# Queries, keys and values of both layers with seven block products instead of eight for some row pairs

## The reference, cut to what matters

```python
for l in range(DEPTH):                                    # two layers
    h = _rms_norm(x, norm_g[l])
    proj = jnp.einsum('bsd,de->bse', h, w_in[l])          # 256 x 2048 times 2048 x 6208
    q_a, k_a, v_a, z_a, c_q, c_kv, k_r, z_b = jnp.split(proj, split_points, axis=-1)
    ...                                                   # q_a, k_a, v_a: 1024 columns each
    o_a = _diff_attention(qa, ka, va, lam, rel_bias_table)
    ...
    x = x + jnp.einsum('bse,ed->bsd', mixed, w_out[l])
return second_block(...)
```

## Time and profile before

| | |
|---|---|
| median of 3 runs | 1946.02 us (1945.85 to 1946.25) |
| profiled execution | 1946.43 us |
| its span in the profile | 1944.6 us |
| PE matmul busy | 1928.8 us, 99% |
| DVE busy | 1371.4 us, 71% |
| ACT busy | 1047.4 us, 54% |
| granted TensorE clock, mean | 0.998 |

### The profile page before, as it was taken

The page is one execution under the profiler, slowest core; times in us unless marked ns, Lnnn a source line. Parts: engine busy times, 40 slices in busy tenths (PEclk is TensorE's granted clock), DMA queues, the critical chain, the costliest instruction groups (busy, mean ns, idle before and its releaser), DMA issues.

```text
span 1944.6 us, 27002 instructions
## 1 busy us (share of the span) xinstructions
PE 1928.8 (99%) x9818; PEld 1635.5 (84%) x9818; DVE 1371.4 (71%) x1941; ACT 1047.4 (54%) x1533; POOL 46.4 (2%) x73
## 2 busy tenths in 40 slices
PE   8999999999999999999999999999999999999997
PEld 7888888888888888888888888888888888888886
DVE  7755675656655675656768766888877887888787
ACT  5533676654433676664544544555555555555554
POOL 1000030000000020000100000000000000000000
PEclk9999999999999999999999999999999999999999
DMA  8666545556666555545666545565656566676653
GB/s 310 205 194 194 151 145 160 151 157 186 187 194 192 146 162 174 153 151 180 213 193 188 158 164 186 182 193 184 194 185 193 185 189 188 191 240 203 219 188 117
DMA packets 246964, 357.06 MB, mean 184 GB/s; under 512 B 15318, under 2 KB 136496, under 8 KB 246364
## 3 DMA queue, kind: packets, MB, share of 16 engines
q1 hardware_dynamic: 245148, 349.08, 58.3%
q0 software_dynamic: 1584, 6.54, 1.0%
q10 hardware_dynamic: 144, 0.26, 0.0%
HBM read 352.69 MB, written 3.16 MB: 183 GB/s over the span
## 4 chain that ended last, share of the span: by engine, by line
PE 98%; DMA 1%; DVE 1%; ACT 0%; issue 0%; SPq 0%; ACTq 0%
PE acc L410 22%; PE acc L387 16%; PE acc L389 15%; PE acc L388 15%; PE acc L403 11%; PE acc L1249 3%; PE acc L1250 3%; PE acc L1248 3%; PE aux L467 2%; PE aux L964 1%; DMA sb_stage<-w_kv 1%; PE aux L1249 1%; PE aux L1250 1%; PE aux L1248 1%; PE aux L982 1%; PE aux L945 1%
## 5 line engine op out<-in xcount | busy, mean ns | idle before, releaser
L350 DVE TENSOR_TENSOR sb_w_lo<-sb_stage,sb_w_hi 128x1024 fp32r<-128x1024 f32 x567 | 694.3, 1227 | 377.0 <-ACT sb_w_hi L345 369.9
L345 ACT ACTIVATE sb_w_hi<-sb_stage 128x1024 fp32r<-128x1024 f32 x567 | 598.5, 1058 | 501.5 <-PE acc L389 248.9
L410 PE MATMUL acc<-sb_xT,sb_w_hi 128*128 128x512 f32 x1856 | 445.7, 391 | 0.0
L410 PEld LDWEIGHTS acc<-sb_xT,sb_w_hi 128*128 128x128 f32 x1856 | 340.8, 188 | 65.8
L387 PE MATMUL acc<-sb_w_hi,sb_xT 128*128 128x512 f32 x768 | 305.7, 398 | 0.0
L389 PE MATMUL acc<-sb_w_hi,sb_xT 128*128 128x512 f32 x768 | 299.5, 390 | 0.0
L388 PE MATMUL acc<-sb_w_lo,sb_xT 128*128 128x512 f32 x768 | 299.3, 390 | 0.0
L403 PEld LDWEIGHTS acc<-sb_xT,sb_w_lo 128*128 128x128 f32 x1856 | 238.7, 191 | 9.3
L403 PE MATMUL acc<-sb_xT,sb_w_lo 128*128 128x256 f32 x1856 | 243.0, 283 | 0.0
L387 PE MATMUL acc<-sb_w_hi,sb_mT 128*128 128x512 f32 x560 | 224.7, 401 | 0.8 <-DVE sb_mT L490 0.7
L389 PE MATMUL acc<-sb_w_hi,sb_mT 128*128 128x512 f32 x560 | 218.6, 390 | 0.0
(11 more groups left out here) (335 smaller groups left out, 1910.5 us busy)
## 6 DMA issues: line engine op xcount, KB each, us to landing
sb_stage<-w_in SPq DMA_DIRECT2D x248, 512.0 KB, 3.9
sb_stage<-w_up SPq DMA_DIRECT2D x176, 512.0 KB, 3.7
sb_stage<-w_out SPq DMA_DIRECT2D x96, 512.0 KB, 4.2
sb_stage<-w_down SPq DMA_DIRECT2D x60, 512.0 KB, 7.0
sb_pair_stage<-w_down SPq DMA_DIRECT2D x28, 512.0 KB, 6.9
sb_stage<-w_kv SPq DMA_DIRECT2D x16, 512.0 KB, 6.8
sb_stage<-w_ukv SPq DMA_DIRECT2D x16, 512.0 KB, 4.0
sb_stage<-w_uq SPq DMA_DIRECT2D x12, 512.0 KB, 3.6
```

The costliest lines, as they stand in the source:

```text
L345: act.activation(w_hi[:, j % RING, 0:size], stage[:, j % RING, 0:size], ACT.Copy).then_inc(hi_ready, 1)
L350: dve.tensor_tensor(w_lo[:, j % RING, 0:size], stage[:, j % RING, 0:size], w_hi[:, j % RING, 0:size].bitcast(F32), ALU.subtract).then_inc( ...
L410: mm = pe.matmul(acc[:, 2 * pair + c, :], hi[:, k, c * P:(c + 1) * P], both, start=first and k == 0, stop=last and k == 3)
```

## The change

In each third (queries, keys, values: 1024 columns, two chunks) some row pairs are multiplied as a 2x2 block product in Winograd's form: the blocks of the left side are row tile x token block, those of the right side row tile x 512 columns. In the first third pairs 0 and 1 go this way, in the other two pairs 0, 1 and 2; that is 8 of 24 per layer. Such a "seven" takes the place of two ordinary units (one in each chunk) and is four units long in the counters: `seven0` to `seven3`, with 2, 1, 2 and 2 block products of three passes each. There are then 64 units in the stage, of which 32 are ordinary ("rows").

- New on SP: the weights of a seven are loaded by two DMAs of 512 KB into one of two pair slots (in `kvb`).
- New on DVE: four sums of 128x512 weights for each seven; `mix_x`, the sums of x blocks, 3 times 7 instructions per layer, placed in the memory stage before layer 0 and in the output projection before layer 1; `add_sevens_qkv` once and `add_rows_qkv` twice per third, in place of two `evacuate_scaled`.
- New on ACT: a copy of `m_first` per third, and `scale_qkv` (two instructions per chunk), since DVE no longer applies the norm's factor.
- Units of this stage are prepared five ahead, in six slots (two of them in `mT`). The last ones are prepared three ahead again.
- The loop over keys and values is written out.
- PE waits at a seven for `mixed_ready`, `tb_free` and `m_free`, and after the stage for `m_free` and `qkv_scaled`.

```diff
+QKV_ITEMS = [[[2, 3, 4], 0, [5], 1, [6, 7]]] + 2 * [[[3, 4], 0, [5], 1, [6], 2, [7]]]
...
+def qkv_ahead(u):
+
+    first = {0: [3], 1: [4], 2: [5], 3: [6, 7], 4: [8, 9]}
+    last = {U_QKV - 5: [], U_QKV - 4: [], U_QKV - 3: [U_QKV], U_QKV - 2: [U_QKV + 1], U_QKV - 1: [U_QKV + 2]}
+    return first.get(u, last.get(u, [u + QKV_RING - 1]))
...
+        def round_qkv(act, layer, j):
...
+            if kind == "seven2":
+                act.wait_ge(qkv_sums_ready, 2 * n + 1)
+            if kind == "seven3":
+                act.wait_ge(qkv_sums_ready, 2 * n + 2)
+            act.wait_ge(unit_used, base + max(0, j - QKV_RING + 1))
...
+        def rest_qkv(step, dve, layer, j):
...
+            dve.tensor_tensor(lo, src, hi.bitcast(F32), ALU.subtract).then_inc(lo_ready, 1)
+            if QKV[j][0] == "seven1":
...
+                dve.wait_ge(lo_ready, base + (j + 1))
+                step(dve.tensor_tensor(b11, b11, b12, ALU.add))
+                dve.tensor_tensor(b12, b12, b22, ALU.add).then_inc(qkv_sums_ready, 1)
+                dve.wait_ge(qkv_sums_ready, 2 * n + 1)
+                step(dve.tensor_tensor(b22, b11, b22, ALU.add))
+                dve.tensor_tensor(b21, b22, b21, ALU.add).then_inc(qkv_sums_ready, 1)
...
+                    def load_qkv_pair(n):
...
+                        if n >= 2:
+                            sp.wait_ge(lo_ready, base + (QKV_SEVENS[n - 2] + 4))
...
+                    def qkv_seven(j):
...
+                        pe.wait_ge(lo_ready, base + (j + 1))
+                        qkv_passes(m_first, near(0, 0), j, 0, first, last)
+                        qkv_passes(acc[:, 2, :], mixed(2), j, 1).then_inc(unit_used, 1)
+                        pe.wait_ge(lo_ready, base + (j + 2))
+                        qkv_passes(acc[:, 0, :], near(1, 0), j + 1, 0).then_inc(unit_used, 1)
+                        pe.wait_ge(lo_ready, base + (j + 3))
+                        qkv_passes(m_fifth, mixed(0), j + 2, 0, first, last)
+                        qkv_passes(m_seventh, mixed(3), j + 2, 1, first, last).then_inc(unit_used, 1)
+                        pe.wait_ge(lo_ready, base + (j + 4))
+                        qkv_passes(m_sixth, mixed(1), j + 3, 0, first, last)
+                        qkv_passes(acc[:, 1, :], near(1, 1), j + 3, 1).then_inc(unit_used, 1)
...
+                    def add_sevens_qkv(third):
+                        dve.wait_ge(m_copied, 3 * layer + third + 1)
+                        step(dve.tensor_tensor(inner_f, m_sixth, qkv_part(2 * third, 0), ALU.subtract))
+                        step(dve.tensor_tensor(outer_f, inner_f, m_seventh, ALU.subtract))
+                        dve.tensor_tensor(qkv_part(2 * third + 1, 0), m_fifth, inner_f, ALU.add)
+                        dve.tensor_tensor(qkv_part(2 * third + 1, 1), m_fifth, outer_f, ALU.add).then_inc(m_free, 1)
...
+                    for j in range(U_QKV):
+                        if j - 1 in QKV_END:
+                            add_rows_qkv(QKV_END.index(j - 1))
+                        if j - 4 in QKV_LAST_SEVEN:
...
+                            add_sevens_qkv(third)
+                        for ahead in qkv_ahead(j):
...
                         if j in (2, 3):
                             turn_scale(dve, tb0 + (j - 2), gain0 + (j - 2), par[:, bass.ds(layer * KT + 12, 4)])
                             turn_rest(dve, turn0 + (j - 2), token_part(xT, 3, j - 2, 0), token_part(xT, 3, j - 2, 1))
                         if j == 4:
                             x_rstd(step, dve, layer * SQ_PRO + SQ_PRO)
```

More of the change, by code:

```diff
@@ L73 @@
 U_MEM = 16
[L74 removed]
+U_QKV = 64
+U_LAYER = U_QKV + 32 + 32 + 32
 U_MIX = 14 * 4
@@ L149, with qkv_units @@
 DOWN_RING = 6
+QKV_ITEMS = [[[2, 3, 4], 0, [5], 1, [6, 7]]] + 2 * [[[3, 4], 0, [5], 1, [6], 2, [7]]]
+QKV_MIXED = 3
+def qkv_units():
+    units = []
+    for third, items in enumerate(QKV_ITEMS):
+        for item in items:
+            if isinstance(item, list):
+                units += [("rows", k, 2 * third + half) for half in range(2) for k in item]
+            else:
+                units += [(f"seven{part}", item, third) for part in range(4)]
+    return units
+QKV = qkv_units()
+QKV_RING = 6
+QKV_ROWS = [j for j, unit in enumerate(QKV) if unit[0] == "rows"]
+QKV_SEVENS = [j for j, unit in enumerate(QKV) if unit[0] == "seven0"]
+QKV_BEGIN = [min(j for j in QKV_ROWS if QKV[j][2] == c) for c in range(6)]
+QKV_END = [max(j for j in QKV_ROWS if QKV[j][2] == c) for c in range(6)]
+QKV_FIRST_SEVEN = [min(j for j in QKV_SEVENS if QKV[j][2] == third) for third in range(3)]
+QKV_LAST_SEVEN = [max(j for j in QKV_SEVENS if QKV[j][2] == third) for third in range(3)]
+assert len(QKV) == U_QKV and len(QKV_ROWS) % RING == 0 and (U_QKV - RING) % QKV_RING == 0
+UNSTAGED = (U_QKV - len(QKV_ROWS)) // RING
+def qkv_ahead(u):
+    first = {0: [3], 1: [4], 2: [5], 3: [6, 7], 4: [8, 9]}
+    last = {U_QKV - 5: [], U_QKV - 4: [], U_QKV - 3: [U_QKV], U_QKV - 2: [U_QKV + 1], U_QKV - 1: [U_QKV + 2]}
+    return first.get(u, last.get(u, [u + QKV_RING - 1]))
 def sevens_until(j):
@@ new lines, in qkv_nth, with qkv_parts @@
+        def qkv_nth(j):
+            return sum(first <= j for first in QKV_SEVENS) - 1
+        def qkv_parts(j):
+            kind = QKV[j][0]
+            hi, lo = qkv_slot(j)
+            if kind == "rows":
+                return stage[:, QKV_ROWS.index(j) % RING, :], hi, lo
+            pair = qkv_pair(qkv_nth(j))
+            by_part = lambda ap: ap.rearrange("p (k n) -> p k n", n=512)
+            if kind == "seven0":
+                return pair[:, 0, :], hi, lo
+            if kind == "seven1":
+                return pair[:, 1, 512:UNIT], hi[:, 0:512], lo[:, 0:512]
+            return pair[:, :, 0:512] if kind == "seven2" else pair[:, :, 512:UNIT], by_part(hi), by_part(lo)
@@ L728, in _ @@
[L728 to L735, removed]
+                            load(sp, base, U_QKV + 8 * c + i, rows(w_in, KT, i, 2, COL_CQ + c * 512), 512,
+                                 QKV_ROWS[i - RING] if c == 0 and i < RING else None)
@@ L1859, in _ @@
                         c, i = u // 8, u % 8
+                        if layer + 1 < LAYERS and (c, i) in ((2, 5), (3, 0), (3, 5)):
+                            mix_x(((2, 5), (3, 0), (3, 5)).index((c, i)), gain0 + (10 if i == 5 and c == 3 else 8))
                         if c > 0 and i in (2, 3):
```

278 lines of the change are left out of this document (198 added, 80 removed).

## The result

The changed kernel takes 1949.61 us (median of 17 runs, 1948.83 to 1950.38); the kernel before, in the same rounds, 1946.08 us (17 runs, 1945.33 to 1947.86). The ratio is 1.0018, with a 95% interval of 1.0011 to 1.0025: slower by about 3.5 us. The forecast was 1943.4 us, the range 1938.5 to 1948.5, so the time lies outside it, and on the side that had 0.14.

The account below looks back on a forecast made before the run. PE's matmul issue was taken as the bound: 48 fewer matmuls (-10.9 us) plus 8.3 us of stalls gave -2.6 us; with the median 0.4 below the profiled execution, the forecast was 1943.4 us, range 1938.5 to 1948.5.

Parts of the forecast that it names:

- the side that had 0.14: Chance given to a time slower than forecast: late pair loads 0.07 and a late low-rank stage 0.07.
- Costed at nothing: Work priced at zero: mix_x under 5.1 us a block, hidden in DVE's idle time; also ACT's additions and the loads.
- Entry: Start of each layer's stage: unit 10's split late in DVE's queue, PE stalls 1.9 us, plus 0.1 for the stall.
- Keys to values: End of the keys: banks read out late behind sums and a split, PE stalls 1.1 us, plus 0.1.
- Values to the low-rank stage: End of the values: PE wants banks at 5.44, DVE reads them until 6.24; stall 0.85 us, plus 0.1.
- the walk: Step-by-step timing of DVE's queue at the stage's critical places: 4.15 us of stalls a layer, 8.3 in all.
- From queries to keys: no stall: End of the queries: four rows behind the last seven instead of two, 5.4 us more, so no PE stall.
- The rule weighed: Semaphores between chained DVE instructions cost nothing extra: 1.7 us less, 1941.7 us; rejected for the rows' 0.12 us per wait.
- 1: Rival: DVE keeps up everywhere in the stage, no stalls; -10.9 us, 1935.1 us; chance 0.10.
- rival 2: The stalls are there but about half as long: 2 to 7 us, time 1937 to 1942 us; chance 0.22.
- 3, late pair loads: SP's queue, six sevens a layer: pairs take over 12.2 us to land; at 14 us each, 1965 us; chance 0.07.
- 4, the low-rank stage starting late: DVE and ACT start it behind, PE waits in the heads; 0.8 us in 16 heads gives 1956 us; chance 0.07.

Follow-up runs that it names:

- the three edits: Changed kernel with readout ahead of the split, norm's factor at unit 18 and layer 0's third block of x sums at unit 22: 1943.37 us, 0.9986.

## Why the prediction was wrong

**The gain** was right: 48 matmuls at 0.2267. By PE's pace a stage without any stall would take 564 x 0.2267 + 1.0 = 128.86 us. Layer 1 took 5.54 more than that, layer 0 9.61, together 15.2; the forecast had 8.3, and the gain is 10.9. Hence +4.3 by the windows, where -2.6 was forecast. Of the 6.9 us above the forecast's stalls 4.1 are `mix_x`'s, 2.6 are small sizes and 0.2 the three stalls. (The prediction's "some 129 us" for the stage is this time without stalls; by its own sum it should have read 133.)

**The step that failed: "Costed at nothing", `mix_x`.** It was given a price that holds (at most 5.1 us a block; 2.97 measured), and then hidden behind "DVE idles 377 us before 567 splits". That is an average over the whole program. The three blocks of layer 0 stand in a stage where DVE also turns x, reads out the memory's projections and computes a factor, and there it has hardly any idle time. The same paragraph named the price without that cover, "up to 2 us at three places a layer", and put it into neither the sum nor the range. Leaving the blocks out gave back 4.3 us, all that layer 0 had lost beyond layer 1, and its 1945.3 us lies inside the forecast's range. Yet the forecast gain isn't there either: 1945.3 is 1.9 us above the forecast, and not told apart from the kernel before. The blocks of layer 1 lie in the output projection of layer 0, and cost nothing visible: from window to window PE takes 310.10 us, as before. The view to read was DVE's timeline of this stretch in the kernel before. From 45.34 to 59.1 us it has no gap, and up to 70 us it has four:

```profile
60.43 1.23 DVE L350 TENSOR_TENSOR sb_w_lo<-sb_stage,sb_w_hi 128x1024 fp32r<-128x1024 f32 x1 [1.27 <-ACT sb_w_hi L345]
61.98 1.41 DVE L450 TENSOR_SCALAR sb_qa<-acc,sb_rstd_m 128x512 f32<-128x512 f32 x2 [0.32 <-PE acc L389]
...
65.85 1.23 DVE L350 TENSOR_TENSOR sb_w_lo<-sb_stage,sb_w_hi 128x1024 fp32r<-128x1024 f32 x1 [1.32 <-ACT sb_w_hi L345]
...
68.66 1.23 DVE L350 TENSOR_TENSOR sb_w_lo<-sb_stage,sb_w_hi 128x1024 fp32r<-128x1024 f32 x1 [0.92 <-ACT sb_w_hi L345]
```

That is 3.8 us of cover for 8.9 us of new work, 5.1 short. The loss was 4.1; the two need not be equal, since splits prepared ahead hide a part.

**The three stalls** stood where they were forecast, in both layers. Entry: 1.77 and 0.13 in the unit behind it, against 1.9 + 0.1. Keys to values: 1.42 + 0.13 against 1.2. Values to the low-rank stage: 0.78 against 0.95. That is 4.2 us where the walk said 4.15. The causes are shown as well, one by one: the factor (moved away, the entry's wait is gone), the readout behind a split (swapped, the wait behind unit 63 is gone and 0.26 us is left behind unit 41), and the sums in the entry's queue (shrunk, its wait is gone in layer 1). There the entry's wait goes by either of two edits; it takes both the sums and the factor to make DVE late.

**Small sizes off.** Layer 1 has 1.3 us beyond the three stalls. About 0.8 of it is the slower pace in the sevens (4.86 us, where 4.76 was forecast: "a seven there costs PE only its matmuls" did not carry over), 0.4 stands at units 8, 19 and 20, and 0.13 at the unit behind the last stall. "From queries to keys: no stall" was thus off by 0.3 a layer. There ACT waits for a row load, which I had called four rows ahead:

```profile
546.95 1.06 ACT L799 ACTIVATE sb_w_hi<-sb_stage 128x1024 fp32r<-128x1024 f32 x1 [2.32 <-DMA sb_stage<-w_in]
```

Issuing the pair loads later left it as it was, so why these loads are late stays open. Nor are they shown to be the cause: with the sums shrunk ACT waits as long (2.43 us at 541.11), and PE loses nothing at units 19 and 20.

**The rule weighed** (the Trainium skill, VectorE: DVE Perf Modes, "The DRAIN you can't avoid") would have made the sums shorter. They start 0.73 apart here as well (522.98, 523.70, 524.43 and 525.16 in layer 1), and from seven 6's first split to the second block's scaling, the stretch with the sums, the walk's 4.66 us came out at 4.65 (521.11 to 525.76), so the rows were right to decide.

**The rivals.** 1 and 2, fewer stalls, are excluded by PE's waits: the three forecast places alone cost about 8.5 us of extra time in the two layers, and rival 2 had at most 7. 3, late pair loads: ACT waits for none of them in this stage. 4, the low-rank stage starting late: between the two windows the distance is 310.10 us, and before it was 506.16 - 196.06 = 310.10 as well; nothing. The slower side came by a path that I had not made a rival of.

**Part of the range.** Its upper end, 14 us of stalls, came from one more microsecond at each of the six known places. The 4 us came from other places, units 0 to 7 of layer 0, with a cause of their own, which no such margin covers. The whole came to 15.2.

## What to carry to other kernels

Idle time that is to hide new work must be read in the window where the work will stand, engine by engine; a program's total says nothing of it. Here the prologue was the fullest stretch. Where PE's pace is the bound and a helper engine takes over more work, walk its queue at every place where PE wants something of it; that walk came out within 0.1 to 0.35 us here. If a stall appears, first look whether the step PE waits for can change places with one that nobody waits for: two such swaps and one block on another engine turned 3.5 us of loss into 5.4 us of gain.

## What the runs showed of the hardware that was not expected

- In four of the profiled executions (the factor moved, one row pair at the opening, the three edits, and those with later pair loads) PE's granted clock fell to the 1.2 GHz level (0.50 to 0.55 in windows of 3 us) once, near a wait: of 1.95, 2.82, 2.17 and 2.15 us. Three times the fall came 0.9 to 1.5 us after the wait had ended, and once 0.6 before its end. It cost 1.3 to 1.6 us beyond the 0.13 to 0.17 that the unit behind a wait loses anyway. None of the waits up to 1.8 us in these stages was followed by it (1.78 with the third block of sums moved, 1.80 in layer 1 with the factor moved). But the wait of 2.83 us behind unit 20 in layer 0, in the kernel with one row pair at the opening, was not either, so the length alone does not decide; the rest is open.
- GpSimd and DVE were slower in places where they ran together: two splits took 3.70 us instead of 2.35, a subtraction of 0.68 us took 1.78, and GpSimd's 128x128 subtraction 0.46 or 1.33, with DVE busy each time. The block of sums of x, seven instructions, took 2.97 us on DVE and 7.6 on GpSimd.
- A wait costs more than itself: the recorded 1.57 us behind unit 9 moved the next unit's start by 1.77, and the unit behind such a wait was another 0.13 to 0.17 us longer than its matmuls, 0.11 of it at the first (0.34 us to the next start, as at 534.01).
- The same matmuls of 128x512 started 0.2267 us apart in the rows and 0.231 apart in the sevens of this stage.
